# First six norms: the squares' sum by one all-ones product of 128 columns, root and reciprocal on 512 columns

## The reference

```python
def rmsnorm(x, g):
    xf = x.astype(jnp.float32)
    y = xf * lax.rsqrt(jnp.mean(xf * xf, axis=-1, keepdims=True) + EPS)
    return (y * g.astype(jnp.float32)).astype(x.dtype)

for l in range(DEPTH):                                  # DEPTH = 2
    x = x + 0.5 * swiglu(rmsnorm(x, ln_ffn1[l]), w_ffn1_gu[l], w_ffn1_down[l])
    h = rmsnorm(x, ln_mix[l])
    z = h @ w_in[l]
    ...
    x = x + (g_pool * a + g_attn * b) @ w_out[l]
    x = x + 0.5 * swiglu(rmsnorm(x, ln_ffn2[l]), w_ffn2_gu[l], w_ffn2_down[l])
```

## Time and profile before

| | |
|---|---|
| median of three runs | 4164.63 us |
| the profiled execution's own time | 4164.48 us |
| its span | 4162.7 us |
| TensorE matmuls busy | 4091.2 us, 98% of the span |
| VectorE, ScalarE, GpSimd busy | 1999.9, 1449.5, 1882.9 us |
| mean granted TensorE clock | 0.994 |
| instructions of the first six norms' sums and spreads on TensorE | 48 + 48 |

### The profile page before, as it was taken

How to read it: one execution, slowest core, us unless ns; L and a number is a source line. 1 busy time by engine, 2 the same in 40 slices (tenths; PEclk the granted TensorE clock), 3 DMA queues, 4 the chain that set the end, 5 groups by cost and what they waited for, 6 DMA issues and landing times.

```text
span 4162.7 us, 52854 instructions
## 1 busy us (share of the span) xinstructions
PE 4091.2 (98%) x19412; PEld 3387.7 (81%) x19412; DVE 1999.9 (48%) x3492; ACT 1449.5 (35%) x2182; POOL 1882.9 (45%) x1408
## 2 busy tenths in 40 slices
PE   8999999999999999999998999999999999999998
PEld 7888778888888877888776998888888888888887
DVE  3212553211220453321258554498789946666653
ACT  3222243222322333322323433333577742222222
POOL 4444334444444434444432534455433345555553
PEclk9999999999999999999999999999999999999999
DMA  3222122222222212222210002233455575555542
GB/s 135 97 101 94 71 71 91 96 96 91 101 100 93 93 61 84 98 91 101 97 70 32 1 11 102 91 138 136 148 206 205 206 249 190 200 193 193 188 172 81
DMA packets 134662, 486.50 MB, mean 117 GB/s; under 512 B 8704, under 2 KB 74496, under 8 KB 92032
## 3 DMA queue, kind: packets, MB, share of 16 engines
q1 hardware_dynamic: 49392, 351.29, 23.5%
q10 hardware_dynamic: 85136, 133.38, 9.2%
HBM read 417.54 MB, written 67.11 MB: 116 GB/s over the span
## 4 chain that ended last, share of the span: by engine, by line
PE 43%; issue 32%; POOL 21%; DVE 3%; ACT 0%; POOLq 0%; ACTq 0%; DVEq 0%
POOL w_lo L442 21%; PE bank L1106 12%; PE bank L1107 12%; PE bank L1108 12%; PE bank L1933 1%; PE bank L1694 1%; PE bank L1710 1%; PE bank L1706 1%; DVE gv L2345 0%; DVE gk L2345 0%; DVE gq L2345 0%; PE bank L1868 0%; DVE p_t L2369 0%; PE bank L1663 0%; PE bank L1614 0%
## 5 line engine op out<-in xcount | busy, mean ns | idle before, releaser
L442 POOL TENSOR_TENSOR w_lo<-raw,w_hi 128x512 fp32r<-128x512 f32 x1324 | 1782.8, 1378 | 2124.0 <-ACT w_hi L545 2123.9
L1106 PE MATMUL bank<-h_hi,w_hi 128*128 128x512 f32 x3232 | 1272.4, 394 | 19.5 <-DVE h_lo L2060 10.5
L1107 PE MATMUL bank<-h_lo,w_hi 128*128 128x512 f32 x3232 | 1261.2, 390 | 0.0
L1108 PE MATMUL bank<-h_hi,w_lo 128*128 128x512 f32 x3232 | 1260.5, 390 | 0.0
L545 ACT ACTIVATE w_hi<-raw 128x2048 fp32r<-128x2048 f32 x331 | 632.7, 1912 | 1054.1 <-PE bank L1108 1020.3
L1106 PEld LDWEIGHTS bank<-h_hi,w_hi 128*128 128x128 f32 x3232 | 608.9, 188 | 151.8 <-POOL w_lo L442 16.5
L1108 PEld LDWEIGHTS bank<-h_hi,w_lo 128*128 128x128 f32 x3232 | 608.2, 188 | 128.4
L1107 PEld LDWEIGHTS bank<-h_lo,w_hi 128*128 128x128 f32 x3232 | 609.0, 188 | 123.7 <-issue 1.5
L1106 PE MATMUL bank<-w_mix_hi,w_hi 128*128 128x512 f32 x1024 | 398.4, 389 | 0.9 <-ACT stage L910 0.9
L1108 PE MATMUL bank<-w_mix_hi,w_lo 128*128 128x512 f32 x1024 | 398.4, 389 | 0.0
L1107 PE MATMUL bank<-w_mix_lo,w_hi 128*128 128x512 f32 x1024 | 398.4, 389 | 0.0
(11 more groups left out here) (376 smaller groups left out, 4496.0 us busy)
## 6 DMA issues: line engine op xcount, KB each, us to landing
raw<-weights SPq DMA_DIRECT2D x331, 1024.0 KB, 4.8
g_store<-g_buf ACTq DMA_DIRECT2D x8, 4096.0 KB, 18.3
g_in<-g_store ACTq DMA_DIRECT2D x32, 1024.0 KB, 5.5
s_store<-stage ACTq DMA_DIRECT2D x60, 512.0 KB, 2.9
s_in<-s_store ACTq DMA_DIRECT2D x30, 1024.0 KB, 7.5
x<-x_in SPq DMA_DIRECT2D x4, 512.0 KB, 7.9
out<-x SPq DMA_DIRECT2D x8, 256.0 KB, 2.2
keys_sb<-keys ACTq DMA_DIRECT2D x1, 1024.0 KB, 4.8
```

Of the source, the lines that this page charges most:

```text
L442: pool.tensor_tensor(w_lo[:, slot, cols], raw[:, slot, cols], w_hi[:, slot, cols].bitcast(F32), ALU.subtract).then_inc(lo_written, 1)
L1106: pe.matmul(out_ap, w_hi[:, slot, cols], m_hi, start=start, stop=False)
L1107: pe.matmul(out_ap, w_hi[:, slot, cols], m_lo, start=False, stop=False)
L1108: return pe.matmul(out_ap, w_lo[:, slot, cols], m_hi, start=False, stop=stop)
```

## The change

For k = 0 to 5 the sum is one fp32 matmul with the all-ones 128x128 matrix as weights and the 512 columns of squares as moving operand, into bank 5 or 7. Each of the 128 output partitions then holds the sums of all 512 tokens. ScalarE reads the bank and writes sqrt(sum/1024 + EPS) to `rstd`, VectorE replaces it by its reciprocal in place. The four matmuls of the sum, VectorE's scaling, the four matmuls of the spread and the copy from the bank go. Norms 6, 7 and 8 stay as they are, with their semaphore counts shifted by six. EPS becomes a column in memory, written once at the start.

```diff
+        eps = place("eps", [P, 1], F32)
...
+        COLUMN_NORMS = 6
+        def norm_bank(k):
+            return 7 if k in (1, 4, 6) else 5
...
                 split_hi(tile + 2)
-                act.wait_ge(sem("variance_written"), k + 1)
-                c_std.up(act.activation(rcol[:, 1, :], rcol[:, 0, :], ACT.Sqrt))
+                if k < COLUMN_NORMS:
+                    act.wait_ge(sem("squares_summed"), k + 1)
+                    c_std.up(act.activation(rstd[:, :], banks[norm_bank(k)][:, :], ACT.Sqrt, scale=1.0 / D, bias=eps[:, 0:1]))
+                else:
+                    act.wait_ge(sem("variance_written"), k - COLUMN_NORMS + 1)
+                    c_std.up(act.activation(rcol[:, 1, :], rcol[:, 0, :], ACT.Sqrt))
...
-                if 0 < k < 8:
+                if 0 < k < COLUMN_NORMS:
+                    pe.wait_ge(sem("x_updated"), KB * k)
+                elif 0 < k < 8:
                     pe.wait_ge(sem("x_updated"), KB * (k - 1) + 2)
+                if k < COLUMN_NORMS:
+                    c_stat.up(pe.matmul(banks[norm_bank(k)][:, :], ones, total, start=True, stop=True))
+                    return
...
             def spread_rstd(k, bank):
-                pe.wait_ge(sem("rcol_written"), k + 1)
+                if k < COLUMN_NORMS:
+                    return
+                pe.wait_ge(sem("rcol_written"), k - COLUMN_NORMS + 1)
...
-                        if first and n == 1:
-                            pe.wait_ge(sem("variance_written"), k + 1)
...
+            local.step(dve.memset(eps[:, :], EPS))
...
                 between()
+                if k < COLUMN_NORMS:
+                    dve.wait_ge(sem("deviation_written"), k + 1)
+                    c_rstd.step(dve.reciprocal(rstd[:, :], rstd[:, :]))
+                    return
                 dve.wait_ge(sem("squares_summed"), k + 1)
```

More of the change, by code:

```diff
@@ L2085, in norm_operand @@
                 c_rcol.step(dve.reciprocal(rcol[:, 2, :], rcol[:, 1, :]))
-                dve.wait_ge(sem("rstd_spread"), k + 1)
+                dve.wait_ge(sem("rstd_spread"), k - COLUMN_NORMS + 1)
                 c_rstd.step(dve.tensor_copy(rstd[:, :], banks[7 if k in (1, 4, 6) else 5][:, :]))
```

## The result

The changed kernel is slower. Its median is 4193.97 us (4190.93 to 4196.55, 4 runs), against 4164.74 (4162.9 to 4168.65, 4 runs) for the kernel before: a ratio of 1.0069, with a 95% interval of 1.0051 to 1.0086. I had forecast 4158.8 us and a range of 4155 to 4165. The profiled execution's span is 4189.7 us, 27.0 more than before, at a granted clock of 0.995 against 0.994.

A forecast was written before the change was run, and what follows sets the result against it. TensorE, busy 98% of the span, was taken as the bound, with the norms' chain covered. Six norms giving back 0.95 us each make 5.7 us: 4164.48 - 5.7 = 4158.8 us, own range 4156 to 4161.5, 8 in 10 within 4155 to 4165.

The forecast's parts named there:

- The other edits cost nothing: Writing the EPS column, at the start while VectorE waits for x, and the remaining edits were given no cost.
- TensorE's pace of 0.227 us: On TensorE, each matmul step taken as 0.227 us, from 48 matmuls of one tile in 10.88 us.
- The added product: On TensorE in each of six norms, one fp32 128x512 product: 0.86 us, 1.32 us from matmul before to second behind.
- A norm's gain: On TensorE, sum and spread go (1.80 us), the product comes (0.86): 0.95 us back per norm.
- The reciprocal: On VectorE over 512 columns: 3.37 us by the slope of 4 to 40 columns; bounds 0.69 and 6.56.
- `rstd`: End of the norm's chain in norm 1: ready at 395.46, 0.19 us before today's.
- Its cover: `rstd` may come 0.95 us later (mixer) or 0.93 (FFN) than today; reciprocal up to 4.5 us before TensorE waits.
- The total of the norms: Six norms at 0.95 us each on TensorE: 5.7 us saved, 3.7 to 8.6 us by the product's bounds.
- D: Rival, chance 0.03: reciprocal's slope steeper than at 4 to 40 columns, TensorE waits; 4171.3 us at the doubled slope.
- A: Rival, chance 0.06: VectorE's long reciprocal waits for GpSimd at the port and is slower; nearly all gain lost, 4163.9 us.
- B: Rival, chance 0.09: TensorE comes earlier but the next weight or activation isn't there, gain given back; 4164.5 us.
- C: Rival, chance 0.07: product costs less than in the head swaps, nearby matmuls at pace; 1.35 us a norm, 4156.3 us.

The follow-up runs named there:

- e2: The kernel before with an unused hole of 32 bytes ahead of gain, where the change puts its EPS column, nothing else: 4200.95 us, ratio 1.0085.
- e1: The changed kernel with the EPS column in rcol's 16 spare bytes, every other buffer where it lay before: 4160.96 us, ratio 0.9991 to the kernel before.
- f3: The changed kernel with EPS in rcol's spare bytes and holes of 128 bytes ahead of gates, 160 ahead of m_row: 4152.43 us, ratio 0.9967 to before.
- g1: The kernel before, old norms, with holes of 128 bytes ahead of gates and 160 ahead of the second mixer's m_row: 4158.5 us, ratio 0.9984.
- e4: The kernel before with act_hi and act_lo alone moved by 32 bytes: 4179.43 us, ratio 1.0034.
- f1: The kernel before with w_hi and w_lo moved by 128 bytes against all other buffers, which keep their place modulo 512: 4237.2 us, ratio 1.0172.
- f2: The kernel before with every buffer from x on moved by 128 bytes: 4164.9 us, ratio 0.9996.
- f4: The kernel before with act_hi and act_lo alone moved by 128 bytes: 4177.93 us, ratio 1.0031.
- g4: The kernel before with the weights' low part alone moved by 128 bytes against everything else: 4224.94 us, one run.
- g2: The kernel before with act_hi and act_lo alone moved by 64 bytes: 4167.91 us, one run.
- e3: The kernel before with an unused hole of 64 bytes ahead of gain, where the change puts its EPS column: 4177.14 us, ratio 1.0026.
- g3: The kernel before with act_hi and act_lo alone moved by 192 bytes: 4175.86 us, one run.

## Why the prediction was wrong

**The step that failed** is "The other edits cost nothing: the column of EPS is written while VectorE waits for x". I asked only when the column is written, and put nothing on its place. It stands ahead of act and w_mix in the order of buffers and puts them 32 bytes off. Measured by e2, that alone costs 35.7 us; by the changed kernel against e1, 33.0. The sum should have had a term of 5184 * 6.6 ns = 34.2 us. With it the forecast is 4158.8 + 34.2 = 4193.0, and 4193.97 was measured.

**What made it invisible to me:** I took TensorE's pace of 0.227 us as a constant of the matmul. The groups of the kernel before had 389 ns for w_mix and 395 to 400 for att, y and mix_late side by side, the same matmul by shape and type. I had the rows before me and put nothing on them.

**The steps that held.** The added product: 1.32 us over three starts, as said. A norm's gain: 0.95 said, 0.91 to 1.01 behind the four norms of an FFN. The reciprocal: 3.37 us by the slope of 4 to 40 columns, 3.35 measured, six times. Against it I had set the Trainium skill, "VectorE: DVE Perf Modes", section "First, the fixed hardware budget", which gives the reciprocal a repeat count of 8. Read as 8 cycles a column, that made an estimate of 4.41 us, and the measurement decides against that reading. `rstd`: 0.19 us earlier said, 0.33 found. Its cover held, and no wait names it. The total of the norms: 5.7 us said, 5.4 and 4.3 by the times (f3 against g1; e1 against before, whose interval reaches from 0 to 7.5), and 4.2 by the traces of f3 and g1. So the sign and the price of one norm hold, while the sum over six came out about a quarter lower in the traces; what is missing lies in the mixers' stretches.

**The rivals.** None was the one that came. D had the right sign with the wrong mechanism: the reciprocal is not slower than its slope. (Its sum had a slip too: 6 * 1.11 is 6.7 us and not 6.8.) A did not come: the reciprocal ran beside GpSimd's low parts (390.44 to 395.46 in norm 1) in its 3.35 us. B did not come behind the norms of an FFN, as their gains show; behind those of a mixer it can't be told from the stretch's own changes of 1.5 us. C is refuted by the 1.32 us.

**Shown and open.** Shown by moving one thing at a time (e2, e4, f1, f2, f4): the pace of a 512-column fp32r matmul here depends on the distance between the addresses of its moving operand and of the weights, modulo 256, not on either address alone. The period of 256 bytes is seen at two distances: 0, which is fast at 0 and at 256 modulo 512 (226.7 to 227.4 ns), and 128, which is slow at 128 and at 384 (232.4 to 233.3). The work of the other engines has no part in it: the w_mix matmuls that stream while ScalarE, VectorE and GpSimd have no instruction of over 100 ns running come 233.4 ns apart in the changed kernel (504 of them) and 226.7 in the kernel before (439), the same as the rest. Not shown: what in the chip this comes from. g4 fits neither of the two simple readings alone, the weights in the array or those being loaded, but does fit both together. Since it moved the low weights against the activations and against the high weights at once, it can't tell whether the distance between the two sets of weights counts by itself. And all weights in these kernels lie in blocks of 512 bytes, so what another step would do wasn't tried.

## What to carry to other kernels

A new buffer, however small, is an edit of every address behind it: put it into bytes that are free, or at the end, and compare the addresses of before and after ahead of any timing. If a matmul of one shape and type shows two durations in the same kernel, ask where its operands lie; here, to bring all streamed operands to the weights' place modulo 256 was worth 7.6 us of 4166 (interval 2.9 to 10.4) for two unused holes. And a gain of 0.1% in a stage can't be read from the total of a kernel whose addresses changed with it: cut the span at marks that both kernels have.

## What the runs showed of the hardware that I had not expected

The pace of a 128x512 fp32r matmul between others of its kind, by the distance of the moving operand from the weights modulo 256:

| distance, bytes | ns to the next start | where |
|---|---|---|
| 0 | 226.7 | act, before |
| 32 | 233.3 | act, after |
| 64 | 228.9 (231.7, 225.9, 229.2) | act, g2 and e3 |
| 96 | 233.4 (231, 232, 237) | second mixer's y, before |
| 128 | 233.3 or 232.4 | act, f4, and att, before; h, act and w_mix, f1 |
| 160 | 234.3 | att, after |
| 192 | 233.3 | act, g3; att, e3 |
| 224 | 233.4 | second mixer's y, f1 |

Only one of eight places is fast for all three matmuls, and the others cost some 3% of a matmul, 64 the least. Steps of 1 ns in this table do not rank the places: att, at the same addresses, has 233.3 ns in the kernel before and 232.4 in g3. The granted clock was 0.993 to 0.995 in all these profiles, so the clock has no part in it.
